# The delta rule's block inverse: the untransposed copy made by VectorE's 32x32 transposes of the transposed one

## What is computed

```python
a = jnp.where(strict, jnp.einsum('bhnid,bhnjd->bhnij', k_beta, k) * decay, 0.0)
rhs = jnp.concatenate([v * beta[..., None], k_beta * jnp.exp(cum)[..., None]], axis=-1)
sol = lax.linalg.triangular_solve(a + eye, rhs, left_side=True, lower=True, unit_diagonal=True)
```

## Time and profile before

| | before |
|---|---|
| median of three executions | 4295.78 us |
| the profiled execution | 4293.81 us |
| its span in the trace | 4291.9 us |
| mean granted TensorE clock | 0.942 of 2.4 GHz |
| matmuls, weight loads | 25559 each |

### The profile page before, as it was taken

How to read it: one execution, slowest core, us unless ns; L and a number is a source line. 1 busy time by engine, 2 the same in 40 slices (tenths; PEclk the granted TensorE clock), 3 DMA queues, 4 the chain that set the end, 5 groups by cost and what they waited for, 6 DMA issues and landing times.

```text
span 4291.9 us, 62567 instructions
## 1 busy us (share of the span) xinstructions
PE 3921.9 (91%) x25559; PEld 3622.3 (84%) x25559; DVE 2567.2 (60%) x5015; ACT 1553.1 (36%) x2769; POOL 758.1 (18%) x613
## 2 busy tenths in 40 slices
PE   7999989889979999998999999999889999978999
PEld 5667869789969999896888888888789998977999
DVE  4654328899959999997455555555452433555342
ACT  4544223345533333333433323332342424444231
POOL 0000005466722332331111110111000001110000
PEclk9999999999989999998789999999889998988999
DMA  3112324358879999994001101010022211112222
GB/s 112 56 61 68 98 69 139 126 177 282 269 236 323 334 332 327 320 331 155 26 26 35 35 30 40 30 35 26 30 85 88 89 64 50 60 40 69 87 92 69
DMA packets 203069, 528.19 MB, mean 123 GB/s; under 512 B 17032, under 2 KB 91272, under 8 KB 202784
## 3 DMA queue, kind: packets, MB, share of 16 engines
q1 hardware_dynamic: 99792, 341.22, 23.8%
q0 software_dynamic: 37440, 136.33, 9.1%
q10 hardware_dynamic: 65552, 46.64, 3.5%
HBM read 477.99 MB, written 46.14 MB: 122 GB/s over the span
## 4 chain that ended last, share of the span: by engine, by line
PE 65%; DVE 23%; ACT 6%; issue 4%; DMA 1%; POOL 0%; DVEq 0%; ACTq 0%; POOLq 0%; SPq 0%
PE bank L94 64%; DVE wl L121 4%; DVE acc L131 3%; DVE H L121 2%; ACT wh L115 2%; DVE row L163 2%; DVE yc L131 1%; DVE eq L121 1%; PE bank L97 1%; DMA raw<-in_v 1%; DVE aal L121 1%; DVE fs L121 1%; DVE sq L131 1%; ACT Xh L115 1%; DVE Xl L121 1%
## 5 line engine op out<-in xcount | busy, mean ns | idle before, releaser
L94 PE MATMUL bank<-Xh,wh 128*128 128x272 f32 (+3 forms) x3680 | 1244.9, 338 | 60.8 <-ACT ft L115 25.5
L94 PE MATMUL bank<-Xl,wh 128*128 128x272 f32 (+3 forms) x3680 | 1173.2, 319 | 0.0
L94 PE MATMUL bank<-Xh,wl 128*128 128x272 f32 (+3 forms) x3680 | 1170.7, 318 | 0.0
L121 DVE TENSOR_TENSOR wl<-raw,wh 128x1024 fp32r<-128x1024 f32 (+1 forms) x536 | 576.1, 1093 | 477.7 <-ACT wh L115 476.5
L115 ACT ACTIVATE wh<-raw 128x1024 fp32r<-128x1024 f32 (+1 forms) x632 | 589.1, 953 | 703.2 <-PE bank L94 660.5
L94 PEld LDWEIGHTS bank<-Xh,wh 128*128 128x128 f32 x3680 | 719.3, 195 | 132.4 <-issue 66.0
L94 PEld LDWEIGHTS bank<-Xl,wh 128*128 128x128 f32 x3680 | 720.8, 196 | 18.6 <-issue 2.4
L94 PEld LDWEIGHTS bank<-Xh,wl 128*128 128x128 f32 x3680 | 717.8, 195 | 20.8
L121 DVE TENSOR_TENSOR H<-H,bank 128x384 f32<-128x384 f32 (+3 forms) x522 | 252.4, 490 | 353.6 <-PE bank L94 350.0
L94 PE MATMUL bank<-aah,wh 128*128 128x384 f32 x1024 | 356.4, 348 | 43.3 <-DVE wl L121 23.5
L121 POOL TENSOR_TENSOR wl<-raw,wh 128x1024 fp32r<-128x1024 f32 x96 | 273.6, 2852 | 517.2 <-ACT wh L115 516.9
(11 more groups left out here) (305 smaller groups left out, 6469.8 us busy)
## 6 DMA issues: line engine op xcount, KB each, us to landing
raw<-in_u SPq DMA_DIRECT2D x128, 512.0 KB, 4.0
raw<-in_v SPq DMA_DIRECT2D x128, 512.0 KB, 5.9
raw<-in_up SPq DMA_DIRECT2D x64, 512.0 KB, 3.6
raw<-in_down SPq DMA_DIRECT2D x64, 512.0 KB, 3.5
scratch<-gb ACTq DMA_DIRECT2D x12, 2048.0 KB, 13.8
gj<-scratch SPq DMA_DIRECT2D x32, 768.0 KB, 7.3
raw<-in_w_gdn SPq DMA_DIRECT2D x48, 512.0 KB, 3.5
raw<-in_w_att SPq DMA_DIRECT2D x36, 512.0 KB, 3.5
```

The lines of the kernel that those rows point to most:

```text
L94: return Issued(self, self.q and self.q.matmul(out, l, r, start=start, stop=stop), 1)
L121: return Issued(self, self.q and self.q.tensor_tensor(out, a, b, op), 1)
```

## The change

TA is no longer updated on its own. After each update of TB, at levels 1 to 4, VectorE writes TA as the blockwise transpose of TB: each 32x32 square is transposed in its place, all 128x384 of a group in one instruction. The same instruction makes TA at level 0. The products pd with their banks and VectorE's subtractions into TA go, as do level 0's transposes on TensorE and copies on ScalarE. Level 0 has no step of its own in the merge any more (no `yield`): its three groups are put into the queue with level 1's first x, and `levels_gdn` counts 42 steps.

```diff
+    def squares(self, out, in_):
+        return Issued(self, self.q and self.q.transpose(out, in_), 1)
...
             for g in range(3):
-                PA.take(("lev0", p, g))
                 do("level0", p, g)
-                PA.give(("lev0", p, g), ("ta0", p, g))
-                yield 1
             for lv in range(1, 6):
...
                 for g in range(3):
-                    if lv < 5:
-                        PA.take(("pd", p, lv, g))
-                        PA.give(("pd", p, lv, g), ("ta", p, lv, g))
                     PA.take(("pt", p, lv, g))
                     do("level_t", p, lv, g)
...
-                streams.append((levels_gdn(t - 1), 45))
+                streams.append((levels_gdn(t - 1), 42))
```

On TensorE, `level0` is gone and `level_t` keeps only pt, with the same waits. ScalarE's `level0` is gone. VectorE:

```diff
             def level_t(p, lv, g):
                 b = 1 << lv
-                if lv == 1:
-                    dv.wait_ge("ta0", p, g)
-                if lv < 5:
-                    dv.wait_ge("dmm", p, lv, g)
-                    less("pd", "dmm", TA, 0).then_inc("ta", p, lv, g)
-                dv.wait_ge("tmm", p, lv, g)
-                less("pt", "tmm", TB.at[p], b).then_inc("tb", p, lv, g)
+                pt = PS[PA.at["pt", p, lv, g]][:, 0:192].rearrange("p (m r) -> p m r", r=b)
+                tb = three(TB.at[p], g).rearrange("p c x -> p (c x)")
+                to = cols_of(tb, lv, b)
+                dv.wait_ge("tmm", p, lv, g)
+                dv.tt(to, to, pt, ALU.subtract).then_inc("tb", p, lv, g)
+                if lv < 5:
+                    dv.wait_ge("tb", p, lv, g)
+                    dv.squares(three(TA, g).rearrange("p c x -> p (c x)"), tb).then_inc("ta", p, lv, g)
+
+            def level0(p, g):
+                dv.wait_ge("qe", p, g)
+                dv.wait_ge("tb0", p, g)
+                dv.squares(three(TA, g).rearrange("p c x -> p (c x)"),
+                           three(TB.at[p], g).rearrange("p c x -> p (c x)")).then_inc("ta0", p, g)
```

More of the change, by code:

```diff
@@ L1858, in keys_out @@
                 i.then_inc("ktr", p, g)
[L1860 to L1865, removed]
             def level_x(p, lv, g):
@@ L1880, in level_t @@
                 b = 1 << lv
-                def part(key, lhs, rhs, o):
-                    ps = PS[clear(pe, PA, (key, p, lv, g))]
-                    pe.wait_ge("x", p, lv, g)
-                    if lv == 1:
[L1886 to L1892, removed]
-                if lv < 5:
-                    part("pd", lambda n: TB.at[p][:, 3 * g + n, :], lambda n: x[:, n, :], 0).then_inc("dmm", p, lv, g)
-                part("pt", lambda n: x[:, n, :], lambda n: TB.at[p][:, 3 * g + n, :], b).then_inc("tmm", p, lv, g)
+                ps = PS[clear(pe, PA, ("pt", p, lv, g))]
+                pe.wait_ge("x", p, lv, g)
+                if lv == 1:
+                    pe.wait_ge("tb0", p, g)
+                else:
+                    pe.wait_ge("tb", p, lv - 1, g)
+                for n in range(3):
+                    i = pe.mm(ps[:, n * 64:n * 64 + 64].rearrange("p (m r) -> p m r", r=b),
+                              x[:, n, :], cols_of(TB.at[p][:, 3 * g + n, :], lv, b))
+                i.then_inc("tmm", p, lv, g)
             def scan_r(p, c):
@@ L2003, in pe_program @@
                 onehot=onehot, ba=ba,
-                gdn_dup=gdn_dup, decay=decay, pair_kk=pair_kk, pair_kq=pair_kq, keys_out=keys_out, level0=level0,
+                gdn_dup=gdn_dup, decay=decay, pair_kk=pair_kk, pair_kq=pair_kq, keys_out=keys_out,
                 level_x=level_x, level_t=level_t, scan_r=scan_r, scan_v=scan_v, scan_s=scan_s, ml_if=ml_if,
@@ L2499, in dv_program @@
                 gdn_exp=gdn_exp, conv=conv, l2=l2, decay=decay, pair_kk=pair_kk, pair_kq=pair_kq, keys_out=keys_out,
-                level_x=level_x, level_t=level_t, scan_r=scan_r, scan_s=scan_s, gdn_gate=gdn_gate,
+                level0=level0, level_x=level_x, level_t=level_t, scan_r=scan_r, scan_s=scan_s, gdn_gate=gdn_gate,
                 gdn_split=gdn_split, gw_split=gw_split, gw_bias=gw_bias, ml_if=ml_if, ml_softplus=ml_softplus, ml_logf=ml_logf,
@@ L2789, in pair_kk @@
                 ac.act(three(DD.at[p], g), three(DD.at[p], g), ACT.Exp).then_inc("dd_exp", p, g)
[L2791 to L2794, removed]
             def scan_v(p, c):
@@ L2893, in ac_program @@
                 gdn_exp=gdn_exp, gdn_take=gdn_take, conv_v=conv_v, conv_qk=conv_qk, decay=decay, pair_kk=pair_kk,
-                level0=level0, scan_v=scan_v, scan_s=scan_s, gdn_split=gdn_split,
+                scan_v=scan_v, scan_s=scan_s, gdn_split=gdn_split,
                 ml_load=ml_load, gw_split=gw_split, ml_if=ml_if, ml_softplus=ml_softplus, ml_dup=ml_dup, ml_exp=ml_exp,
```

## The result

The changed kernel takes 4282.95 us (median of 9 runs, 4256.59 to 4289.52), the kernel before 4297.06 (9 runs): ratio 0.9956, interval 0.9939 to 0.9973. That is 14 us less, where 42 were forecast, and just above the range of 4222 to 4280.

What follows compares the result with a forecast made beforehand. TensorE was taken as the bound. Terms: -71 us of products, +25.5 from six waits for ta with their clock loss less the sq wait, +3 of chain, sum -42.5: 4252 us from 4293.8, range 4222 to 4280.

Steps and rivals of the forecast that it cites:

- The products: On TensorE, the inverse's pd products (64.5 us) and level 0's transposes (6.5 us) go: 71 us less.
- + 3: Longer chain inside a level, from pt through subtraction and transpose to the next product: 0 to 10 us, 3 taken.
- The transposes: 120 new VectorE transposes of 128x384, taken at 0.555 us each; VectorE then at 60%, not a bound on average.
- The rival of a slow transpose: VectorE's queue at level_t: a transpose costs 2.2 us, block by block; 4318 us, slower; chance 0.06.
- The estimate of 0.58: One VectorE transpose of 128x384: the skill's 311 ns for 128x128 plus 256 columns at 1.05 ns.
- The wait for ta: TensorE at the first level_x waits about 3.6 us for level 0's transposes, in six of eight periods.
- the burst: VectorE's convolution, ke, two wl and one ogl ahead of level 0's transposes, placed 0.69 us after keys_out's third product starts.
- The wait for sq of 1.19 us: TensorE's wait right after the first level_x's wait for ta: given back, counted as 1.1 us in six periods.
- The clock: TensorE's slow clock behind each new wait for ta: 1.75 us lost each; without this term, 10.5 us better.
- the old stops: TensorE's waits for ScalarE's squared gated outputs (sq) at full periods' starts; no new clock loss was forecast for them.
- VectorE's bursts eat more: Products behind transposes also wait at later levels: another 3 us in six periods, 8 us of clock; 4278 us; chance 0.19.

Runs made afterwards that it cites:

- e6: e1 with TensorE also issuing the pd products and level-0 transposes, which nothing reads; levels still read VectorE's transposes: 4298.46 us, ratio 1.0009.
- e1: The changed kernel, but level 0 keeps three steps of its own in the merge (45 steps counted, not 42): 4244.61 us, ratio 0.9875.
- e13: The changed kernel with 9 unread products in the middle of each inverse, before its third level: 4259.67 us, ratio 0.9915.
- e5: e1 with the two sums over the gated outputs also one scan step later: 4204.01 us, ratio 0.9781.
- e11: The changed kernel with 9 unread products before each of the eight inverses: 4259.78 us, ratio 0.9919.
- e8: e1 with 9 unread products at the start of each inverse: 4205.42 us, ratio 0.9819.
- e9: The changed kernel with 25 unread products once, ahead of the first inverse alone: 4286.58 us, ratio 0.9971.
- e10: The changed kernel with 50 unread products once, ahead of the first inverse alone: 4291.96 us, ratio 0.9992.
- e15: The kernel before with 9 unread products before each inverse: 4344.02 us, ratio 1.0107.
- e4: The kernel before, with none of the change, but the two sums over the gated outputs one scan step later: 4241.12 us, ratio 0.9883.
- the best: e5 with 9 unread products before each inverse: 4176.42 us, ratio 0.9712.

## Why the prediction was wrong

**The products: right in kind, too low, and lucky in the sum.** Without the clock the sum was -71 + 6 x (3.6 - 1.1) + 3 = -53 us; measured, at 2.4 GHz, -60. Two misses cancel in it: e6 against e1 puts the products at 78 to 85 us where I had 71, and e1 against the changed kernel puts the waits at 27 where I had 15 + 3.

**The transposes: right.** 0.555 taken, 0.573 measured, and e6 shows that VectorE's side costs nothing that can be told. The rival of a slow transpose is out. The estimate of 0.58, worked out from the 311 ns of the Trainium skill (page "VectorE: DVE Perf Modes", section "The three transpose paths"), agrees with the 0.573.

**The wait for ta: right in place and cause, too short.** 3.6 us forecast, 5.2 measured, 33.5 in all for 21.6. What I had wrong is where the burst begins: I took its place from the kernel before; with the level-0 steps gone TensorE comes to it sooner, VectorE doesn't. The wait for sq of 1.19 us behind it is gone, as said. That it is this wait and not another, e1 shows: 27 us come back with it.

**The clock: the step that failed.** The prediction has it as "I add that once per new wait", 1.75 us, 10.5 us in all, and puts the old stops at nothing. Between the profiled executions it cost 55.5. By the lengths of the slow stretches some 10 of these do stand behind the new waits for ta (7 us of low clock behind each, at half speed, where the kernel before had 3 to 4 behind its wait for dd). Some 43 stand behind the old stops for sq, which last as long as before, but are followed by 24 us at 1.2 GHz in place of 3 to 4. The earlier trace rows had the stop, and I read from it a price per stop that I took to hold for the changed kernel too; it held for the kernel before as it stands. (With the 10.5 replaced by the 55.5, and 53 by 60, the sum is -4 us, which is what the profiled executions differ by, 4293.8 and 4289.5; that is so by construction.)

**The rivals.** "VectorE's bursts eat more" gave 4278 us, near what came, but for another reason: of the eight waits for ta only one, of 1.71 us, is at a later level. None of the cases had the clock behind stops that the change doesn't touch, and so the range was too narrow on its upper side.

The nine runs of the changed kernel say the same: the fastest, 4256.59 us, had a clock of 0.937, the slowest, 4289.52, one of 0.929.

**What is open.** That the clock behind the old stops is what the forecast lacked is shown: e13 leaves the stops, nearly all waits and the products as they are and gets 53 of the 55 us back (251.1 for 304.4) with 2 us of unread work a period, and e6 gets it back with TensorE's old stream. Why one stop is followed by 24 us of low clock and another by 3 isn't shown. It isn't the stop's length or the products around it (e1, e5). It isn't the distance from the stop before by itself either: 108.8 us in e5 gave both outcomes, and after some 130 us the changed kernel has a low clock (2546.61) and e11 has none (2534.74). One program also comes out differently from run to run (the changed kernel's clock is 0.929 to 0.937, e8's 0.937 to 0.949), with the same distances by its code. That leaves the place in time of each stop, which e9 and e10 moved only twice and for all stops at once; no run here tests it further.

## What to carry to other kernels

Write down span x granted clock beside every time: it is nearly what an edit did, and the rest is what the clock made of it (e15 shows the limit). Where a stage has regular stops of TensorE of 2 to 3 us, a gain or loss of 1% can't be credited to an edit before the clock of that stage is compared; give a forecast there a clock term of its own, of both signs, as large as a few of the period's slow stretches. Best is to shorten the stop (e4: one step of order, 57 us by the medians, of which some 40 are clock), and a product whose only reader is a blockwise transpose away belongs on an idle VectorE, if its first use isn't right behind a burst of that engine's queue.

## What the chip showed that I had not expected

TensorE, busy for 24 us without a gap (24.00 of 24.00 us in some periods), ran all of them at the 1.2 GHz level, and in others of the same program at 2.4 GHz after 3 to 4 us. The Trainium skill, page "TensorE: Matmul & The Clock Gate", section "Part 1: The HAM clock gate (the "warmup" mystery)", says that activity releases the slow clock, and counts the penalty of the ramp as under 1% of a typical kernel's span. The first didn't hold here for 24 us of activity (e1, 2647 to 2671 us). For the second, all that the low clock cost is 304.4 of 4287.7 us, 7%, in the changed kernel, and 200.7 of 4180.9, 5%, in the best.
Nine useless products a period made one kernel 39 us faster (e1 to e8) and another 45 us slower (before to e15), by the medians.
